# Expert layer of an encoder on one core: picks joined by diagonal matrices on TensorE, one expert weight loaded earlier, the residual handed on by 512 columns

## The reference

```
x = x + g1 * (concat[A, B] @ w_out)
h = rms_norm(x, norm2_g) * (1 + sc2) + sh2
x = x + g2 * hmoe(h)
return rms_norm(x, final_g)

# hmoe: softmax over 4 groups, take the best; softmax over its 8 experts, take the best two
#   hid = silu(xb @ w1[e]) * (xb @ w3[e])          w1, w3: 1024 x 512 of each expert
#   y   = (hid @ w2[e]) * weight                   w2: 512 x 1024
#   each token gets the sum of its two weighted expert rows
```

## Time and profile before

| what | value |
|---|---|
| time, median of 3 runs | 1394.71 us (1393.04 to 1396.22) |
| time of the profiled execution | 1393.46 us |
| its span, first to last instruction | 1391.6 us |
| PE busy | 1160.8 us (83%) |
| DVE busy | 424.2 us (30%) |
| ACT busy | 350.2 us (25%) |
| POOL busy | 280.4 us (20%) |
| HBM read and written | 291.58 MB and 25.74 MB, 228 GB/s over the span |

### The profile page before, as it was taken

One profiled execution on the slowest core, in us unless ns is written; L12 is line 12 of the kernel. 1 busy time (PEld: TensorE's weight loads), 2 busy tenths in 40 slices (PEclk: granted clock), 3 DMA queues, 4 the chain that ended last, 5 costly groups with the idle time before them and its releaser, 6 DMA issues.

```text
span 1391.6 us, 29607 instructions
## 1 busy us (share of the span) xinstructions
PE 1160.8 (83%) x13023; PEld 718.6 (52%) x13023; DVE 424.2 (30%) x726; ACT 350.2 (25%) x736; POOL 280.4 (20%) x254
## 2 busy tenths in 40 slices
PE   5899999999997798988799947997888778877750
PEld 3465555555454677877655534554444444444420
DVE  2100043434665554656436360000000000000008
ACT  3200023353333554566521111110010010010004
POOL 0100012221326433467412001111111111111000
PEclk8999999999998999999999968999999999999985
DMA  9895131122345221221407079999999999999965
GB/s 320 289 338 185 59 102 61 53 82 80 142 135 137 55 49 27 49 58 25 169 8 279 39 299 349 390 390 396 397 401 404 405 407 401 397 391 401 413 254 209
DMA packets 82025, 314.74 MB, mean 226 GB/s; under 512 B 13808, under 2 KB 28488, under 8 KB 65150
## 3 DMA queue, kind: packets, MB, share of 16 engines
q1 hardware_dynamic: 75862, 298.96, 57.9%
q0 software_dynamic: 5120, 12.59, 2.6%
q10 hardware_dynamic: 936, 1.61, 0.3%
HBM read 291.58 MB, written 25.74 MB: 228 GB/s over the span
## 4 chain that ended last, share of the span: by engine, by line
PE 28%; DMA 27%; DVE 5%; ACT 5%; issue 3%; SPq 0%; POOL 0%; DVEq 0%; ACTq 0%; POOLq 0%
DMA arena<-in_exp_w 26%; PE bank L1582 10%; PE bank L2450 6%; PE bank L1852 6%; PE bank L2468 2%; PE bank L1606 2%; PE bank L2197 1%; PE bank L2437 1%; DVE arena L1463 1%; DMA arena<-h_scratch,arena 1%; DVE arena L2531 1%; DVE arena L1450 1%; DVE arena L2532 1%; ACT arena L1295 0%; SPq L2306 0%
## 5 line engine op out<-in xcount | busy, mean ns | idle before, releaser
L2450 PE MATMUL bank<-arena 128*64 128x256 f32 x2048 | 259.1, 412 | 67.8 <-DMA arena<-in_exp_w 58.5
L907 PE MATMUL bank<-arena 128*128 128x512 f32 (+1 forms) x736 | 257.3, 498 | 4.2 <-DVE arena L493 2.0
L2450 PEld LDWEIGHTS bank<-arena 128*64 128x64 f32 x2048 | 159.8, 148 | 176.4 <-DMA arena<-in_exp_w 69.7
L1582 PE MATMUL bank<-arena 64*64 64x64 f16 (+3 forms) x7184 | 200.8, 219 | 42.7 <-issue 16.2
L1582 PEld LDWEIGHTS bank<-arena 64*64 64x64 f32 (+2 forms) x7184 | 179.4, 126 | 69.6 <-issue 41.1
L907 PEld LDWEIGHTS bank<-arena 128*128 128x128 f32 x736 | 134.5, 190 | 99.5 <-issue 84.7
L2468 PE MATMUL bank<-arena 128*64 128x512 f32 x512 | 116.9, 598 | 16.6 <-ACT arena L2394 16.6
L2416 DVE TENSOR_TENSOR arena<-bank,arena 128x256 f32<-128x256 f32 x32 | 13.6, 425 | 309.1 <-PE bank L2450 309.1
L2341 POOL DMA_INDIRECT arena<-h_scratch,arena x32 | 30.7, 960 | 370.8 <-PE bank L2437 278.5
L1852 PE MATMUL bank<-arena 128*128 128x512 f32 x192 | 87.9, 607 | 0.0
L2468 PEld LDWEIGHTS bank<-arena 128*64 128x64 f32 x512 | 34.0, 136 | 77.5 <-issue 54.7
(11 more groups left out here) (253 smaller groups left out, 1265.8 us busy)
## 6 DMA issues: line engine op xcount, KB each, us to landing
arena<-in_exp_w SPq DMA_DIRECT2D x96, 2048.0 KB, 44.8
arena<-in_ada_w SPq DMA_DIRECT2D x12, 2048.0 KB
arena<-in_w_in SPq DMA_DIRECT2D x11, 1024.0 KB, 6.5
direction_scratch<-arena SPq DMA_DIRECT2D x6, 1536.0 KB, 5.8
arena<-direction_scratch SPq DMA_DIRECT2D x24, 384.0 KB, 5.5
arena<-pick_out SPq DMA_DIRECT2D x6, 1024.0 KB, 10.3
arena<-in_x_sample SPq DMA_DIRECT2D x8, 512.0 KB, 4.8
arena<-in_w_out SPq DMA_DIRECT2D x8, 512.0 KB, 6.3
```

Of the source, the lines that this page charges most:

```text
L907: return nc.tensor.matmul(bank[i % 3][:, 0:GR[p] * GW], w[:, k, :], hT[:, k, PART[p]], start=(k == 0), stop=(k == KD - 1))
L1582: return nc.tensor.matmul(out, lhsT, r, start=start, stop=True, skip_group_check=True)
L2450: ins = nc.tensor.matmul(bank[b + 2 * c.s][BLK * n:BLK * n + BLK, 0:HALF], xT[c.s][:, j, :], slot[c.w][:, j, n * HALF:(n + 1) * HALF], sta ...
```

## The change

- **Last stage.** For tiles 1 to 5 the weighted sum of the two picks is formed on TensorE: VectorE first makes ten diagonal 128 x 128 matrices from the pick weights (`diag`), and `pe_phase7` multiplies each half of 512 columns of the two picks by its diagonal, accumulating in PSUM (four matmuls of 128 x 128 by 128 x 512 a tile). `join(t)` then multiplies each PSUM half by the gate row and adds the whole to `x2(t)`. ScalarE's `first_row` and the L2531 operation remain for tile 0 alone.
- **Transfers.** The two rows of `w_out` move to P + 2 + 4 * D, so that w2 of slot 1 can be loaded as soon as the first tile's router matmuls are done. SP waits for that (`router_mm` at 1) ahead of h2 row 1. The two loads of `g2_row` move from `sp_phase5` to the place of `f_row`, ahead of it.
- **Residual by halves.** `residual` adds each half of 512 columns right after its multiplication and signals `x2_ready` for each half; `tile_square`, `h2T_evac`, `turned` and `routed` wait for halves. In tile 5 TensorE's order becomes `turned(4)`, five matmuls, `routed(4)`, three matmuls; h2 of tile 5 is formed from x2 times the scale row (before the root is there), then one operation that applies the factor and adds the shift.

```
-wout = [... for a in (dead + W, P + 2 + 5 * TOK, free_kkn, free_v) for j in range(2)]
+wout = [... for a in (dead + W, P + 2 + 4 * D, free_kkn, free_v) for j in range(2)]
...
-def tile_square(act, own, t):
-    act.wait_ge(sem("x2_ready"), t + 1)
+def tile_square(act, own, t, hf):
+    cols = slice(hf * 512, hf * 512 + 512)
+    act.wait_ge(sem("x2_ready"), 2 * t + hf + 1)
+    own.link(nc.scalar.activation(h2[t % 2][:, cols], x2(t)[:, cols], ACT.Square, scale=1.0 / 32.0, accum_out=stat5[:, t, hf:hf + 1]))
+    if hf == 0:
+        own.link(nc.scalar.activation(stat5[:, t, 3:4], stat5[:, t, 0:1], ACT.Identity, bias=eps[:, 0:1]))
+    else:
+        own.done(nc.scalar.activation(stat5[:, t, 3:4], stat5[:, t, 1:2], ACT.Sqrt, bias=stat5[:, t, 3:4]))
...
 # sp_phase5
+            sp.wait_ge(sem("router_mm"), 1)
+            weights(2, 1)
             for t in range(1, NT - 1):
                 h2_rows(t)
 
@@
             weights(0, 1)
             h2_rows(NT - 1)
             weights(1, 1)
-            weights(2, 1)
             weights(0, 2)
...
             weights(1, 2)
-            for g in range(2):
-                sp.dma_start(g2_row[:, g, :], mod_dram[g, 5 * D:6 * D].partition_broadcast(P)).then_inc(sem("g2_in"), 16)
...
 # residual
-                k = own.done(nc.vector.tensor_tensor(tmp[:, cols], out_bank(t, hf), g1_row[group(t)][:, cols], ALU.mult))
-            own.wait(k)
-            dve.wait_ge(sem(f"x5_in{min(t, NT_S)}"), 16 if t < NT_S else 16 * NT_P)
-            nc.vector.tensor_tensor(x2(t), x2(t), tmp, ALU.add).then_inc(sem("x2_ready"), 1)
+                own.link(nc.vector.tensor_tensor(tmp[:, cols], out_bank(t, hf), g1_row[group(t)][:, cols], ALU.mult))
+                if hf == 0:
+                    dve.wait_ge(sem(f"x5_in{min(t, NT_S)}"), 16 if t < NT_S else 16 * NT_P)
+                nc.vector.tensor_tensor(x2(t)[:, cols], x2(t)[:, cols], tmp[:, cols], ALU.add).then_inc(sem("x2_ready"), 1)
...
 # dve_phase5
-                norm(dve, own, t)
+                if t < NT - 1:
+                    norm(dve, own, t)
+            t = NT - 1
+            dve.wait_ge(sem("h2_out0"), 48)
+            dve.wait_ge(sem("x2_ready"), 2 * NT)
+            own.link(nc.vector.tensor_tensor(h2[0], x2(t), ss_row[:, group(t), 1, :], ALU.mult))
+            dve.wait_ge(sem("act_own5"), 4 * NT)
+            own.link(nc.vector.reciprocal(stat5[:, t, 2:3], stat5[:, t, 3:4]))
+            nc.vector.scalar_tensor_tensor(h2[t % 2], h2[0], stat5[:, t, 2:3], ss_row[:, group(t), 0, :], ALU.mult, ALU.add).then_inc(sem("h2_ready"), 1)
             scores(NT - 1)
...
 # pe_phase5
+                if t == NT - 1:
+                    turned(t - 1)
+                    out_part(pe, t, 1, 0, 5)
+                    routed(t - 1)
+                    out_part(pe, t, 1, 5, KD)
+                    break
                 out_part(pe, t, 1, 0, 6 if t == 1 else 3)
...
 # sp_phase6
             sp.wait_ge(sem("y_mm6"), CREDIT + NE - 2)
+            for g in range(2):
+                sp.dma_start(g2_row[:, g, :], mod_dram[g, 5 * D:6 * D].partition_broadcast(P)).then_inc(sem("g2_in"), 16)
             sp.dma_start(f_row, A["final_row"].partition_broadcast(P)).then_inc(sem("final_in"), 16)
...
 # dve_phase7
+            for t in range(1, NT):
+                for k in range(2):
+                    ins = nc.vector.tensor_scalar(diag[:, t - 1, k, :], ident, wts[:, t, k:k + 1], None, ALU.mult)
+            ins.then_inc(sem("diag_ready"), 1)
...
             def join(t):
                 a, b = ya[t][:, 0], ya[t][:, 1]
+                if t:
+                    for hf in range(2):
+                        cols = slice(hf * 512, hf * 512 + 512)
+                        dve.wait_ge(sem("join_mm"), 2 * (t - 1) + hf + 1)
+                        k = own.done(nc.vector.tensor_tensor(a[:, cols], join_bank(t, hf), g2_row[:, group(t), cols], ALU.mult))
+                    own.wait(k)
+                    nc.vector.tensor_tensor(x2(t), x2(t), a, ALU.add).then_inc(sem("joined"), 1)
+                    return
...
+        def pe_phase7(pe):
+            pe.wait_ge(sem("diag_ready"), 1)
+            for t in range(1, NT):
+                pe.wait_ge(sem(f"rows_in{t}"), 16)
+                for hf in range(2):
+                    if t >= 4:
+                        pe.wait_ge(sem("joined"), t - 3)
+                    for k in range(2):
+                        ins = nc.tensor.matmul(join_bank(t, hf), diag[:, t - 1, k, :], ya[t][:, k, hf * 512:hf * 512 + 512], start=(k == 0), stop=(k == 1))
+                    ins.then_inc(sem("join_mm"), 1)
```

More of the change, by code:

```diff
@@ L1103, in build @@
         free_kkn, free_v = at_rkv + 3 * NT * W, at_rkv + 2 * NT * W
-        wout = [arena[:, a + j * D:a + (j + 1) * D] for a in (dead + W, P + 2 + 5 * TOK, free_kkn, free_v) for j in range(2)]
+        wout = [arena[:, a + j * D:a + (j + 1) * D] for a in (dead + W, P + 2 + 4 * D, free_kkn, free_v) for j in range(2)]
         n2_row = arena[:, dead - W:dead + W]
@@ L1416, in act_phase4 @@
                 if n == STEPS:
-                    tile_square(act, own5, 0)
+                    tile_square(act, own5, 0, 0)
+                    tile_square(act, own5, 0, 1)
             squares(whole(STEPS - 1))
             root(whole(STEPS - 1))
-        def tile_square(act, own, t):
-            act.wait_ge(sem("x2_ready"), t + 1)
-            if t:
-                own.wait(own.n)
-            own.link(nc.scalar.activation(h2[t % 2], x2(t), ACT.Square, scale=1.0 / 32.0, accum_out=stat5[:, t, 0:1]))
-            own.done(nc.scalar.activation(stat5[:, t, 1:2], stat5[:, t, 0:1], ACT.Sqrt, bias=eps[:, 0:1]))
+        def tile_square(act, own, t, hf):
[6 more added lines that the diff above has]
+                own.done(nc.scalar.activation(stat5[:, t, 3:4], stat5[:, t, 1:2], ACT.Sqrt, bias=stat5[:, t, 3:4]))
         def rec_bank(i):
@@ L1871, in build @@
         NSLOT = 3
+        assert KH * D == 4 * D
         WEXP = 2 * KD * HID + KH * D
@@ L2011, in act_phase5 @@
                     rec_out(act, NT - 1)
-                h2T_evac(act, t - 1)
-                tile_square(act, own, t)
-            h2T_evac(act, NT - 1)
+                h2T_evac(act, t - 1, 0)
+                h2T_evac(act, t - 1, 1)
+                tile_square(act, own, t, 0)
+                if t == NT - 1:
+                    h2T_evac(act, t, 0)
+                tile_square(act, own, t, 1)
+            h2T_evac(act, NT - 1, 1)
             act.wait_ge(sem("g_centred"), 1)
@@ L2018, in act_phase5, with h2T_evac @@
             nc.scalar.activation(m2, m2, ACT.Exp).then_inc(sem("m_exp"), 1)
-        def h2T_evac(act, t):
-            for hf in range(2):
-                act.wait_ge(sem("h2T_mm"), 2 * t + hf + 1)
-                if t >= 2:
-                    act.wait_ge(sem("router_mm"), t - 1)
-                nc.scalar.copy(h2T[t % 2][:, 4 * hf:4 * hf + 4, :], bank[(4, 7)[hf]].rearrange("p (k c) -> p k c", k=4)).then_inc(sem("h2T_ready"), 1)
+        def h2T_evac(act, t, hf):
+            act.wait_ge(sem("h2T_mm"), 2 * t + hf + 1)
+            if t >= 2:
+                act.wait_ge(sem("router_mm"), t - 1)
+            nc.scalar.copy(h2T[t % 2][:, 4 * hf:4 * hf + 4, :], bank[(4, 7)[hf]].rearrange("p (k c) -> p k c", k=4)).then_inc(sem("h2T_ready"), 1)
         def residual(dve, own, t):
@@ L2036, in residual @@
                 dve.wait_ge(sem("o5_mm"), 2 * t + hf + 1)
[L2037 to L2040 removed]
+                own.link(nc.vector.tensor_tensor(tmp[:, cols], out_bank(t, hf), g1_row[group(t)][:, cols], ALU.mult))
+                if hf == 0:
+                    dve.wait_ge(sem(f"x5_in{min(t, NT_S)}"), 16 if t < NT_S else 16 * NT_P)
+                nc.vector.tensor_tensor(x2(t)[:, cols], x2(t)[:, cols], tmp[:, cols], ALU.add).then_inc(sem("x2_ready"), 1)
         def norm(dve, own, t):
[L2043 removed]
+            dve.wait_ge(sem("act_own5"), 4 * t + 4)
             if t == 0:
                 dve.wait_ge(sem("ss_ready"), 2)
[L2046 removed]
+            own.link(nc.vector.reciprocal(stat5[:, t, 2:3], stat5[:, t, 3:4]))
             own.link(nc.vector.scalar_tensor_tensor(h2[t % 2], x2(t), stat5[:, t, 2:3], ss_row[:, group(t), 1, :], ALU.mult, ALU.mult))
@@ L2178, in turned @@
                 for hf in range(2):
+                    pe.wait_ge(sem("x2_ready"), 2 * j + hf + 1)
                     if j:
@@ L2489, in build, with join_bank @@
         stat7 = take(NT * 4).rearrange("p (t m) -> p t m", t=NT)
+        diag = arena[:, top6:top6 + 2 * (NT - 1) * P].rearrange("p (t k c) -> p t k c", t=NT - 1, k=2)
+        assert top6 + 2 * (NT - 1) * P <= ARENA - 2 * WEXP
+        def join_bank(t, hf):
+            return bank[2 * (t % 4) + hf]
         y_out_v = [O[1][0, t * P:(t + 1) * P, :] for t in range(NT_S)] + [O[0][0, t * P:(t + 1) * P, :] for t in range(NT_P)]
```

15 lines of the change are left out of this document (6 added, 9 removed).

## The result

The changed kernel takes 1381.46 us (median of seven runs, 1376.81 to 1388.28), the kernel before, run beside it, 1393.64 (seven runs, 1389.04 to 1396.22). The ratio, taken run against run, is 0.9931 with a 95% interval of 0.9909 to 0.9952: 9.6 us less, at least 6.7 and at most 12.7. Run once more in the first experiment, the same kernel gave 1383.93 and 0.9929.

A forecast was written before the change was run, and what follows sets the result against it. The prediction took the kernel as bound by the expert weights' stream, beginning at the first reload. Gains of 5.5 us there and 2.3 in the last stage summed to 7.8, giving 1386.9 us, range 1383.6 to 1391.5.

The forecast's parts named there:

- The frame: Expert stage: its end is the first reload's issue, at 848.94, plus a weight stream of fixed length, 87 loads of 2 MB.
- Part 1: Residual by halves and tile 5's tail: scores at 814.0 instead of 815.2, 1.2 us gained, ends 0.4 and 2.0.
- the two legs: Tile 5's tail: VectorE's chain to 813.95 and ScalarE's with the last router passes to 814.0 meet before the scores.
- Part 2: w2 of slot 1 early, gate rows late: gather 3.5 us instead of 7.80; reload 5.5 us earlier, 1.2 from the residual.
- The drain: Second burst ahead of the gather: 8.9 MB take 22 us and end at 832.4, instead of 839.6.
- w2 of slot 2 does not hold the stream: Before the stream: this early load, issued at 836.8, ends at 843.0, ahead of the first reload at 843.4.
- the gather stays slow: First gather: its 7.80 us are its own, not the queue's; gain 1.2 + 2.3 = 3.5, time 1391.2; chance 0.12.
- The gate rows: After the last weights: they land by 1348, before the picks are asked for at 1349.4; priced at nothing.
- The 2 us that the prediction counted on there: Tile 3's residual: about 2 us left though its h2 row lands some 5 us later; if used up, one multiply late.
- Part 3: Last stage, joins on TensorE: final operation ends at 1384.8 against 1387.1, 2.3 us gained, ends 1.8 and 2.8.
- clock stays low: Last stage: TensorE stays at 1.2 GHz throughout, 10.7 us worse there, 5.2 worse in all, 1399.9; chance 0.05.
- The sum: Whole kernel: 5.5 us at the first reload plus 2.3 in the last stage, 7.8 us, giving 1386.9.

The follow-up runs named there:

- the first experiment: The changed kernel repeated with no edit and profiled a second time; 1383.93 us, ratio 0.9929 to the kernel before.
- old residual: Against the changed kernel: residual, squares, norm and router in whole tiles again, with tile 5's former order on TensorE; 1387.59 us, ratio 0.9942 to the kernel before.
- w2 late: Against the changed kernel: only w2 of slot 1 goes back into the burst, the gate rows stay late; 1390.61 us, ratio 0.9972 to the kernel before.
- old transfers: Against the changed kernel: w2 of slot 1 and the two gate rows load where they did before; 1388.15 us, ratio 0.9964 to the kernel before.
- the last run: Changed kernel plus w2 of slot 2 ahead of the list transfers, twelve identity transposes before expert 0, eight matmuls before the picks; 1382.56 us, 0.9913.
- gate rows early: Against the changed kernel: only the gate rows go back into the burst, w2 of slot 1 stays early; 1389.24 us, ratio 0.9961 to the kernel before.

## Why the prediction came out as it did

**The frame held.** The first reload sets the start, and the stream keeps its length: 497.9 to 500.6 us in all fourteen profiles, at the upper end where w2 of slot 2 goes out ahead of the lists. w2's bytes were never saved on the stream.

**Part 1 came out near its 1.2 us: 1.4 at an even clock, 2.3 in the first profiles.** The last multiply was to come 1.7 us later. It came about 1.0 later: from SP's write of h2 row 0 it is 69.94 us in the changed kernel, and 68.9 before without the 1.7 that a fall of the clock took there (70.61 as it stands; below). The working had missed that tile 0's router no longer has its constant row behind the copy: its wait is 0.76 us, before 1.51. From the multiply to the scores 4.6 were forecast and 4.18 came. That makes 2.3 against the profile of before (7.46 - 4.18 - 1.0) and 1.4 against the old residual (6.57 - 4.18 - 1.0); the 0.9 between them is the clock in tile 5's router. The half-by-half order on the two legs was as described; VectorE's leg is the longer by 0.2.

**Part 2: right sum, and partly by luck.** Beside part 1 it was forecast at 4.3 us (5.5 - 1.2); from scores to reload it is 29.70 and 30.61 us in the two profiles, before 33.76: 3.2 to 4.1. The drain came where it was put, 23 us behind the multiply (832.4 - 809.4), but the working had slipped there: a start 1.7 later than 809.5 is 811.2 and not 810.2, which gives 24. The gather was mis-sized: 3.5 us taken, 4.23 by the same chain, 4.1 to 4.4 up to the transposes in all nine runs with nothing ahead of it. The last put was too near a model. An estimate from the Trainium skill, DMA: Bandwidth & Descriptors, section Anatomy of one DMA, 2.6 us, is further off than the 3.5 taken, and the measurement decides. And "w2 of slot 2 does not hold the stream" was wrong (the prediction calls it the eighth early load; it is the ninth): it is still moving when the first reload is issued, so the reload's bytes pass behind it. From scores to reload the sum came out within 0.2 to 1.1 us all the same.

**The rival "the gather stays slow" fell**: 4.2 alone, 6.9 to 11.3 with SP's loads in the engines. The rule of the Trainium skill, DMA: Bandwidth & Descriptors, section Queues, rings and completion order, that an engine takes its queues in turn, agrees with these in kind. The rival's sum was wrong too: without the early load part 1 gives nothing at the first expert, since the landing stays 33.4 to 33.5 us behind the multiply. The parts do not add; the load's early place is what lets part 1 through. By traces, without the early load the gather lands 7.0 us later behind h2 row 0 (839.12 - 735.68 = 103.4, against 828.61 - 732.12 = 96.5), and by the runs the time is 5.7 to 6.0 longer (0.9972 against 0.9931 and 0.9929, with intervals that just overlap).

**The gate rows** cost nothing in their new place, as priced: from the last put to VectorE's first operation of the stage 9.19 us, before 9.26. The early load in the first half cost nothing either: the multiply stands 69.9 behind h2 row 0 with it and without it (w2 late, 69.94). The 2 us that the prediction counted on there are used up, though: tile 3's first multiply waits for the h2 row (5.62 us, put down to that transfer) and comes 1.5 to 1.8 us later behind h2 row 0 than with w2 late (29.09 and 28.75 against 27.25). As forecast, only that one multiply is late; the second comes at the same place (35.36).

**Part 3: 2.3 forecast, 2.2 to 3.7 measured.** The clock stayed at half behind the start of tile 1 for 3.5 us in the changed kernel, 4.8 in the repeat, and up to 6.2 in other runs (5 taken); VectorE's pace behind it is 3.85 a tile (4.0 taken). The rival "clock stays low" fell: 6.2 us at most, against the 25 from which it would have decided.

**The sum.** 5.4 to 6.3 us to the first reload (41.22 - 33.88 and - 34.79, less the 1.0 of the later multiply), less 0.6 to 1.0 of a longer stream, and 3.1 to 3.7 in the last stage: 7.8 to 9.0, where 7.8 were forecast and the runs say 9.6, with 6.7 as their lower end. Of these 0.9 is the clock in tile 5's router of the profile of before, so 6.9 to 8.1 is the change's own by the traces. With both falls of the clock in that profile, this one and the 1.7 below, the two profiles of the changed kernel are 10.7 and 9.5 shorter than it from h2 row 0 to the end; the interval of the runs holds either.

**What stays open.** In the profile of before the granted clock falls to half in tile 1's passes, and takes about 1.7 us (4 us at 0.57); in the changed kernel's it does not:

```profile
741.00:745.00 4.00, 4.00 (x8) 1.74 (x8) 3.90 (x6) 0.00 (x0) 0.23 (x1) 0.57 0.98 414
```

```profile
741.00:745.00 4.00, 4.00 (x12) 1.77 (x11) 3.15 (x6) 1.36 (x5) 0.00 (x0) 1.00 0.96 410
```

The first line is of before, the second of the changed kernel; eight passes stand where twelve fit. The old transfers, the old residual and the last run show the fall too, the first with part 1 in place, so the change does not decide it. How often it happens in either kernel, and with it whether it is part of the 9.6, would take many profiles of each. Nor do the runs part old transfers, w2 late and gate rows early (0.9961 to 0.9972): only the traces order them. The old transfers gained 5.0 us by their runs (2.8 to 7.1), more than the 2.7 that the last stage of their profile shows (30.98 - 28.24), which lies just below that interval; their profiled execution was the slowest of the nine, so part of this may be that execution.

## What to carry to other kernels

Ask of a load that is moved what it gets out of the way of: here 2 MB taken out of a burst saved none of their own 5.2 us, but let a 4.2 us gather, on which the long stream's start hung, run alone. Edits that meet at one landing do not add: measure each with the others in place, and again without. A stage of a few us can be put right by the trace and still not show in runs that spread by 4 to 13 us. A gain seen in one pair of profiles can be a fall of the clock in one of them: look for the same stretch in a third run. And when an early start is won, ask whether the engines still have something to move while it begins.

## What was not expected of the hardware

A small gather is slowed by a load issued behind it as well as by those ahead: of 11.3 us, 1.5 to 1.8 went with the 2 MB load issued 4.8 us later, in one profile of each. A load that starts into empty engines moves little at first: 116 GB/s over 841 to 844, behind an issue at 840.14. And TensorE's clock, 2.4 GHz at 1355, fell to 1.2 at 1356 behind an idle time of only 2.1 us that followed 7 us of passes; passes up to 0.13 us before the picks kept it up.
